# The piece size of sixteen DRAM-to-DRAM transfers in a one-layer decoder kernel on Trainium2: 1152 or 4608 bytes

## The reference, cut to what matters

```python
h = modulate(rms_norm(x, g_ffn1), sh1, sc1)
x = x + 0.5 * (1.0 + gt1) * swiglu(h, w1_ffn1, w3_ffn1, w2_ffn1)

h = modulate(rms_norm(x, g_mix), sh2, sc2)
cq, ckv, kidx, widx, mq, mk, mv, ga, gb = split_cols(h @ w_in)
y_dsa = dsa_attention(...) @ w_proj_dsa
y_moba = moba_attention(mq, mk, mv) @ w_proj_moba
y = sigmoid(ga) * y_dsa + sigmoid(gb) * y_moba
x = x + (1.0 + gt2) * (y @ w_out)

h = modulate(rms_norm(x, g_ffn2), sh3, sc3)
x = x + 0.5 * (1.0 + gt3) * swiglu(h, w1_ffn2, w3_ffn2, w2_ffn2)
return rms_norm(x, g_final)
```

## Time and profile before

| | |
|---|---|
| median of 3 runs | 1116.89 us (1115.84 to 1116.91) |
| the profiled execution's own time | 1115.63 us |
| its span, first to last instruction | 1113.9 us |
| PE busy | 1100.4 us (99%) |
| DVE, ACT, POOL busy | 644.9, 561.7, 201.9 us |
| moved by DMA | 194.44 MB, mean 175 GB/s |

### The profile page before, as it was taken

One profiled execution on the slowest core, in us unless ns is written; L12 is line 12 of the kernel. 1 busy time (PEld: TensorE's weight loads), 2 busy tenths in 40 slices (PEclk: granted clock), 3 DMA queues, 4 the chain that ended last, 5 costly groups with the idle time before them and its releaser, 6 DMA issues.

```text
span 1113.9 us, 16848 instructions
## 1 busy us (share of the span) xinstructions
PE 1100.4 (99%) x6110; PEld 926.8 (83%) x6110; DVE 644.9 (58%) x1068; ACT 561.7 (50%) x1006; POOL 201.9 (18%) x123
## 2 busy tenths in 40 slices
PE   7999999999999999999999999999999999999998
PEld 5678888888888888877778788887899999988887
DVE  5544444444433475659887646677877777742232
ACT  4565656565454344235657654445755555533233
POOL 0055453535443331020101000021000000000000
PEclk9999999999999999999999999999999999999999
DMA  9846654566766637549999923324376666552222
GB/s 330 277 158 194 219 182 156 189 220 216 263 234 232 201 85 229 152 125 234 216 208 202 207 60 100 103 81 161 109 224 179 187 181 182 166 196 92 89 67 77
DMA packets 241106, 194.44 MB, mean 175 GB/s; under 512 B 5671, under 2 KB 238754, under 8 KB 240802
## 3 DMA queue, kind: packets, MB, share of 16 engines
q1 hardware_dynamic: 179760, 127.68, 38.3%
q10 hardware_dynamic: 44786, 47.25, 13.0%
q0 software_dynamic: 16512, 18.87, 10.3%
HBM read 189.59 MB, written 41.94 MB: 208 GB/s over the span
## 4 chain that ended last, share of the span: by engine, by line
PE 91%; DVE 4%; ACT 3%; DMA 1%; issue 1%; SPq 0%; ACTq 0%; DVEq 0%
PE ps L432 22%; PE ps L434 22%; PE ps L433 22%; PE ps L693 5%; PE ps L695 5%; PE ps L694 5%; PE ps L1871 2%; PE ps L1849 1%; PE ps L1836 1%; DMA ada<-in_w_ada 1%; PE ps L1816 1%; DVE w_lo L411 1%; ACT w_hi L406 1%; PE ps L1643 1%; PE ps L1014 1%
## 5 line engine op out<-in xcount | busy, mean ns | idle before, releaser
L411 DVE TENSOR_TENSOR w_lo<-raw,w_hi 128x1024 fp32r<-128x1024 f32 (+1 forms) x128 | 194.1, 1517 | 263.1 <-ACT w_hi L406 262.9
L432 PE MATMUL ps<-h_hi,w_hi 128*128 128x512 f32 x720 | 286.6, 398 | 2.3 <-DVE h_lo L498 2.0
L406 ACT ACTIVATE w_hi<-raw 128x1024 fp32r<-128x1024 f32 (+1 forms) x128 | 145.6, 1138 | 279.2 <-PE ps L434 271.6
L434 PE MATMUL ps<-h_hi,w_lo 128*128 128x512 f32 x720 | 281.2, 391 | 0.0
L433 PE MATMUL ps<-h_lo,w_hi 128*128 128x512 f32 x720 | 280.8, 390 | 0.0
L432 PEld LDWEIGHTS ps<-h_hi,w_hi 128*128 128x128 f32 x720 | 135.3, 188 | 38.0 <-issue 7.4
L434 PEld LDWEIGHTS ps<-h_hi,w_lo 128*128 128x128 f32 x720 | 135.2, 188 | 28.9
L433 PEld LDWEIGHTS ps<-h_lo,w_hi 128*128 128x128 f32 x720 | 135.5, 188 | 26.2 <-issue 0.2
L432 PE MATMUL ps<-g_hi,w_hi 128*128 128x512 f32 x330 | 130.0, 394 | 0.5 <-DVE w_lo L411 0.3
L434 PE MATMUL ps<-g_hi,w_lo 128*128 128x512 f32 x330 | 128.7, 390 | 0.0
L433 PE MATMUL ps<-g_lo,w_hi 128*128 128x512 f32 x330 | 128.6, 390 | 0.0
(11 more groups left out here) (307 smaller groups left out, 1841.9 us busy)
## 6 DMA issues: line engine op xcount, KB each, us to landing
ada<-in_w_ada ACTq DMA_DIRECT2D x27, 1024.0 KB, 5.2
raw<-in_w_ffn SPq DMA_DIRECT2D x24, 1024.0 KB, 5.5
raw<-in_w_ffn SPq DMA_DIRECT2D x16, 1408.0 KB, 6.8
w_s<-in_w_ffn ACTq DMA_DIRECT2D x8, 2304.0 KB, 13.8
s_raw<-w_s SPq DMA_DIRECT2D x72, 256.0 KB, 3.1
raw<-in_w_in SPq DMA_DIRECT2D x64, 256.0 KB, 9.0
w_s<-in_w_ffn POOLq DMA_DIRECT2D x4, 2304.0 KB, 38.3
w_s<-w_s POOLq DMA_DIRECT2D x4, 2304.0 KB, 33.3
```

The costliest lines, as they stand in the source:

```text
L406: nc.scalar.activation(tiles_of(w_hi[j % SPL], nk), raw_of(f, j, nk), ACT.Copy).then_inc(hi_done, 1)
L411: nc.vector.tensor_tensor(tiles_of(w_lo[j % SPL], nk), raw_of(f, j, nk), tiles_of(w_hi[j % SPL], nk).bitcast(F32), ALU.subtract).then_inc( ...
L432: nc.tensor.matmul(ps[:, bank, :], hi, rhs_hi, start=start, stop=False)
L434: return nc.tensor.matmul(ps[:, bank, :], lo, rhs_hi, start=False, stop=stop)
```

## The change

`max_dma_last_dim` caps the size of one contiguous piece of a transfer. It goes from 1152 to 4608 bytes in the eight copies and in the eight accumulating transfers. A row of a quarter becomes one piece in place of four.

```diff
             def accumulate(name, m, src, summed):
-                pool.dma_start(w_sum[m][name], src, accum_op=ALU.add, max_dma_last_dim=1152).then_inc(summed, 16)
+                pool.dma_start(w_sum[m][name], src, accum_op=ALU.add, max_dma_last_dim=4608).then_inc(summed, 16)
...
             src = quarter({"s1": "c", "s2": "a", "s3": "a", "s4": "b"}[name], m)
-            act.dma_start(w_sum[m][name], src, max_dma_last_dim=1152)                .then_inc(first_copied if name in ("s1", "s3") else second_copied, 16)
+            act.dma_start(w_sum[m][name], src, max_dma_last_dim=4608)                .then_inc(first_copied if name in ("s1", "s3") else second_copied, 16)
```

## The result

| | before | after |
|---|---|---|
| median | 1116.56 us (4 runs) | 1158.86 us (4 runs, 1158.68 to 1158.95) |
| span of the profiled execution | 1113.9 us | 1157.0 us |
| PE busy | 1100.4 us | 1110.6 us |

The ratio is 1.0379 with an interval of 1.0365 to 1.0393: slower by 42.3 us, where 38 were forecast.

The account below looks back on a forecast made before the run. PE, busy 99%, bounds the kernel; late gate-weight loads would stall it. One stall of 39 us, less a microsecond for interrupted turns, gives 1116.9 + 38 = 1155 us; other terms 0; range 1122 to 1177.

Parts of the forecast that it names:

- One piece in turn: DMA engines from 495 us: each queue gets one piece in turn, whatever its size, so larger accumulated pieces delay gate-weight loads.
- The turn: Attention stage: one accumulated piece of 4608 bytes plus one load piece takes 0.40 us, bounds 0.27 and 0.46, now 0.127.
- the rival with 1169 us: Accumulated piece grows in proportion to its bytes, 0.444 us; gate loads 49 to 52 us late, up to 1169 us; 20%.
- the one at the lower bound: Accumulated piece takes 0.25 us, 0.27 with a load piece; third gate unit late by 14 us, 1131 us; 16%.
- C, D, E: Gate units whose weights ACT rounds at 522.5, 530.9, 539.9 us; forecast to land at 535, 560.6, 584, PE 7.5, 25, 39 late.
- the pause for s2: POOL waits for s2 before the last two accumulations; in some 5 us without accumulated pieces the backlog of loads goes through.
- The cover of 5 us: After a late weight rounding on ACT, probability copies have about 5 us of slack before PE stands still.
- The sum of 39 us: PE's total delay in the attention stage, set by the third late gate unit: 584 - 539.9 - 5 = 39 us.
- The point from which it decides: A piece-for-piece round of 0.20 us in the attention stage; below that no gate load is late.
- Turns bounded in bytes: Rival: engines let loads move about as many bytes as a 4608-byte piece; 8.1 us a unit or less, 1117 us; 12%.
- The rest: Copies in first feed-forward and at 425 us cost 0 (1.7 without cover); POOL's shorter issue and wait win nothing.
- the last rival: Faster: POOL's and DMA engines' saving reaches PE, whose idle 13.5 us lies nearly all in the first 60; 3%.

## Why the prediction was right, point by point

- **One piece in turn.** Right: 2720 against 2714 pieces after the change, and shown from the other side by doubled transfers.
- **The turn.** 0.40 us was taken, 0.373 measured. A packet of q0 takes 0.082 x 1157.0 x 16 / 4224 = 0.359 us, or 0.371 without the 128 small ones; two passages of a copied piece were estimated at 0.38. The bound in proportion to the bytes, 0.444, was not reached, so the rival with 1169 us falls. So does the one at the lower bound, 1131 us.
- **C, D, E.** Forecast to land at 535, 560.6 and 584; ACT could round them at 539.5, 563.9 and 585.9, all from an execution that runs 0.8 us behind at 481 us. C is late by 4 us, and 2.2 of them are a misread row: the working took the middle of two landings for the second. Before the change C, D and E landed at 514.3, 525.8 and 536.5 us (500.1 + 14.2, 505.6 + 20.2, 511.3 + 25.2), 8, 5 and 3 us early and not 10, 8 and 6. For the rest there are two more turns in a unit, 0.7 us, and the seventh copy, which landed only at 504.0, inside C's turns. The shorter turn gave half of it back until E. The late steps were the right ones, and the pause for s2 ended the stall, as written.
- **The cover of 5 us and the clock.** These are the terms that were mis-sized. The sum of 39 us says how far PE stands behind when E has come. It was right there, as the first matmul of E and the score products after E show, before and after the change:

```profile
548.67 0.39 PE L432 MATMUL ps<-h_hi,w_hi 128*128 128x512 f32 x1
551.48 2.10 PE L1836 MATMUL ps<-mk,mq 64*128 64x256 f32 x12
...
588.30 0.80 PE L432 MATMUL ps<-h_hi,w_hi 128*128 128x512 f32 x1 [9.73 <-DVE w_lo L411]
594.69 2.06 PE L1836 MATMUL ps<-mk,mq 64*128 64x256 f32 x12 [1.29 <-ACT probT L2069]
```

  Less the 0.8 us of this execution, PE is 38.9 us behind at the first and 42.4 at the second, and that stays. What the sum lacks is therefore 3.6 us behind E: its twelve matmuls, ten of them at the lower clock, take 2.3 us longer, and PE waits 1.3 for the copies of probabilities, which the cover of 5 us was to hide. In the forecast's own terms E could be rounded 1.2 us later than 584, and 2.8 us were covered in place of 5. The 10.2 us of slower work and the 32.5 of waits are not an error of +10 beside one of -6: the slow matmuls before E mostly took the place of waiting for it. Only "PE idle by some 39 us" was wrong, it is 32.5. The clock was named only as a possible 5.4 us in the case of 1169. That 38.9 meets 39 so closely is in part luck, since E's landing, the turn and the cover each were off by a little.
- **The point from which it decides.** Wrong. Up to a turn of 0.20 us nothing was to be late; 2304-byte pieces have 0.209 and cost 19.7 us, 1536-byte pieces have 0.155 and cost 8.8 us. The step counted the lateness of C and D alone. Below that point it is the long run that decides: each unit adds what 66 turns exceed PE's interval by, for as long as accumulations are queued, and the interval is 10 us at first and 8 us later.
- **Turns bounded in bytes.** Falls at every size. That is against the reading of the Trainium skill ("DMA: Bandwidth & Descriptors", "SWDGE vs HWDGE vs iDMA") by which a packet near 4096 B would bound a turn: with 4608, 2304, 1536 and 1152 bytes against 512 the counts stay 1 to 1. That an engine goes round its queues, as the Trainium skill says in the same section, agrees with the trace: 1300, 1252 and 1297 pieces of three queues. Pieces above 4608 bytes were not tried.
- **The rest.** The copies in the first feed-forward and at 425 us cost nothing, as said (1116.66 us with large pieces in the copies alone; ACT's wait for `small` is 0.6 us there, 1.7 were worked out). POOL issued its first four transfers in 4.3 us, where three took 8.6. No run shows that this saved wait did harm by itself: q0 had pieces at every turn before the change too. The last two accumulations are issued at 586.0 us in place of 606.6, by about the 20 us that were forecast for their landing. PE's idle time of 13.5 us before the change isn't nearly all in the first 60 us, as the last rival has it: 7.1 us lie there and nearly all of the rest behind 815 us, which changes nothing in the forecast.

One thing stays open: what the lower clock costs in the total. By the rows above it is about 2 us behind E; no kernel was tried that keeps PE busy in its waits.

## What to carry to other kernels

Where a bulk transfer that nobody waits for shares the DMA engines with small loads that someone does wait for, its piece size sets how long every piece of those loads waits (here with 1152 to 4608 bytes against 512). Count turns, (pieces of a load per engine) x (time of the longest round), and hold that against the interval at which the consumer takes loads, at its shortest and over the whole time in which the bulk is queued. If the large pieces are wanted, a wait for each transfer's landing before the next is issued gives the loads their pauses.

## What the runs showed that was not expected

- 256 KB loads in 512-byte pieces took 33 turns each and not 32 (10.25, 13.8 and 24.5 us for a unit at 0.155, 0.209 and 0.373 us a turn).
- Fewer, larger pieces in the accumulation took 8.2% of 1157.0 us in place of 10.3% of 1113.9: 17% less time in the engines for the same bytes, and yet the kernel is 3.8% slower.
- The landing figure of a group of two issues is the middle of the two. An engine that needs both waits for the second, 2.2 to 2.6 us later here before the change.
- Small pieces in a transfer that shares a round with large ones are slow for the same reason: the eighth copy took 52.5 us with 1152-byte pieces and 24.3 us with 4608.
